# Moving half of a normalisation stage, and a bias preparation stage, into the projections beside them

## What is computed

```
for i in range(2):
    h = dilated_mixer(x, ...) if i == 0 else neighbourhood_mixer(x, ...)   # begins with x @ w_qkv
    x = layer_norm(ALPHA * x + h, ln_g[i, 0], ln_b[i, 0])
    f = hierarchical_moe(x, ...)
    x = layer_norm(ALPHA * x + f, ln_g[i, 1], ln_b[i, 1])                  # the closing stage
```

## Time and profile before

| what | us |
|---|---|
| median of 3 runs | 5646.84 |
| lowest and highest | 5639.95, 5656.57 |
| the profiled execution, its own time | 5643.55 |
| its span, first to last instruction | 5641.9 |
| `br`, first DMA issue to the first of `qa` | 12.0 |
| `a_sn`, first load issue to the first of `qb` | 66.6 |

### The profile page before, as it was taken

One profiled execution on the slowest core, in us unless ns is written; L12 is line 12 of the kernel. 1 busy time (PEld: TensorE's weight loads), 2 busy tenths in 40 slices (PEclk: granted clock), 3 DMA queues, 4 the chain that ended last, 5 costly groups with the idle time before them and its releaser, 6 DMA issues. The chain is left out here.

```text
span 5641.9 us, 110382 instructions
## 1 busy us (share of the span) xinstructions
PE 5159.5 (91%) x36030; PEld 4401.6 (78%) x36031; DVE 3861.8 (68%) x6739; ACT 2919.9 (52%) x4917; POOL 1161.2 (21%) x1032
## 2 busy tenths in 40 slices
PE   6999999999899988889999928998999897999993
PEld 5888798988889977778888827988888685888882
DVE  5678887687666658686877647775444555766886
ACT  3343444344388876455656434343777213644774
POOL 2010020000011110054544421100000002543552
PEclk9999999999999999989999969999999897999996
DMA  5877776465599977588988666664544436977996
GB/s 169 214 199 202 197 206 170 133 161 130 146 314 315 315 253 217 178 311 255 343 292 292 223 203 176 199 161 148 155 146 138 141 131 216 318 256 229 364 324 223
DMA packets 867118, 1236.12 MB, mean 219 GB/s; under 512 B 183102, under 2 KB 543981, under 8 KB 866732
## 3 DMA queue, kind: packets, MB, share of 16 engines
q1 hardware_dynamic: 739740, 883.58, 50.5%
q0 software_dynamic: 72272, 276.84, 16.1%
q10 hardware_dynamic: 54720, 70.60, 3.8%
HBM read 916.03 MB, written 333.67 MB: 222 GB/s over the span
## 5 line engine op out<-in xcount | busy, mean ns | idle before, releaser
L522 PE MATMUL qa_ps_out<-qa_x_hi,qa_w_hi 128*128 128x512 f32 x1344 | 534.3, 398 | 40.9 <-DVE qa_w_lo L646 23.8
L522 PE MATMUL qa_ps_out<-qa_x_lo,qa_w_hi 128*128 128x512 f32 x1344 | 529.8, 394 | 0.0
L522 PE MATMUL qa_ps_out<-qa_x_hi,qa_w_lo 128*128 128x512 f32 x1344 | 529.6, 394 | 0.0
L559 ACT ACTIVATE qa_w_hi<-qa_w_whole 128x1024 fp32r<-128x1024 f32 x180 | 191.2, 1062 | 456.9 <-DVE qa_w_whole L637 256.7
L522 PE MATMUL qa_ps_out<-qa_w_hi,qa_x_hi 128*128 128x256 f32 x1344 | 382.4, 284 | 5.6 <-DVE qa_w_lo L646 5.6
L522 PE MATMUL qa_ps_out<-qa_w_lo,qa_x_hi 128*128 128x256 f32 x1344 | 381.1, 284 | 0.0
L522 PE MATMUL qa_ps_out<-qa_w_hi,qa_x_lo 128*128 128x256 f32 x1344 | 381.0, 284 | 0.0
L2613 DVE CUSTOM_DVE_ANT_0 ga_minus_s<-ga_ps_s,ga_bias 128x512 f32<-128x512 f32 (+1 forms) x256 | 194.0, 758 | 257.6 <-PE ga_ps_s L2552 188.6
L1101 ACT ACTIVATE da_prob<-da_minus_s,da_rows 128x256 f32<-128x256 f32 (+1 forms) x768 | 317.9, 465 | 42.6 <-DVE da_rows L1069 42.4
L522 PEld LDWEIGHTS qa_ps_out<-qa_x_hi,qa_w_hi 128*128 128x128 f32 x1344 | 256.3, 191 | 101.0 <-DVE qa_w_lo L646 29.7
L1069 DVE CUSTOM_DVE_ANT_0 da_minus_s<-da_ps_s,da_bias 128x256 f32<-128x256 f32 (+1 forms) x768 | 259.6, 375 | 90.3 <-PE da_ps_s L1000 81.5
(11 more groups left out here) (490 smaller groups left out, 15427.3 us busy)
## 6 DMA issues: line engine op xcount, KB each, us to landing
a_ex_w_raw<-w SPq DMA_DIRECT2D x128, 1024.0 KB, 10.2
b_ex_w_raw<-w SPq DMA_DIRECT2D x128, 1024.0 KB, 10.3
qa_w_raw<-w_qkv_a SPq DMA_DIRECT2D x144, 512.0 KB, 4.2
a_ex_w_raw<-w POOLq DMA_DIRECT2D x66, 1024.0 KB, 9.8
b_ex_w_raw<-w POOLq DMA_DIRECT2D x66, 1024.0 KB, 8.2
da_q_cross<-qT SPq DMA_DIRECT2D x48, 1024.0 KB, 8.0
da_k_parts<-kT SPq DMA_DIRECT2D x48, 1024.0 KB, 10.2
a_mn_o_in<-o SPq DMA_DIRECT2D x16, 1584.0 KB, 8.6
```

The costliest lines, as they stand in the source:

```text
L522: done = pe.matmul(out, stationary, moving, start=(k == 0 and i == 0), stop=(k == KH - 1 and i == 2))
L559: act.activation(w_hi[:, p % W_RING], src, ACT.Copy).then_inc(w_hi_done, 1)
```

## The change

Four edits. (1) The stage `bias_rows` is gone; its two loads, three products, three copies and its store are done at the head of `qa`, with the projection's own result buffers `part` and `ps_out` as space; the first ScalarE copy into `part` waits for the store, and so does `diagonal_bias`. (2) In both projections two tiles are loaded and split ahead of the first weight block, the others behind it, on SP, ScalarE and VectorE. (3) `a_sn` does only the 8 tiles that pass 0 of `qb` reads; the 8 others are done within pass 0 of `qb`, one every three products from product 6 on, in the idle `x_rows`, through a ring of two slots; GpSimd issues their loads and stores and SP waits for the last store before it loads the first tile of pass 1. (4) In `merge_and_norm` `hi(0)` goes ahead of the last part of `w_o` (ahead of the last two in `b_mn`), and `lo(0)` stands right behind the first part.

```diff
+        def late_tile(p, step):
+            if not late or p < LATE_FIRST + step or (p - LATE_FIRST - step) % LATE_EVERY:
+                return None
+            i = (p - LATE_FIRST - step) // LATE_EVERY
+            return i if i < LATE else None
...
+                def late_load(i):
+                    rows = late.sums[bass.ts(late.tiles[i], P), :]
+                    pool.dma_start(late_rows[i % LATE_RING], rows).then_inc(late_loaded[i % LATE_RING], 16)
+
+                def norm_late_rows():
+                    pool.memset(late_power[:], -0.5).then_inc(late_ready, 1)
+                    pool.wait_ge(x_turned, TILES_OF_PASS)
+                    late_load(0)
+                    pool.dma_start(late_gain, row_broadcast(late.gain)).then_inc(late_const, 16)
+                    pool.dma_start(late_shift, row_broadcast(late.shift)).then_inc(late_const, 16)
+                    for i in range(1, LATE_RING):
+                        late_load(i)
+                    pool.wait_ge(late_ready, 1)
+                    for i in range(LATE):
+                        pool.wait_ge(late_widened, i + 1)
+                        pool.tensor_tensor(late_guess[:, i % 2], late_var[:, i % 2], late_power[:], ALU.pow
+                                           ).then_inc(late_guessed, 1)
+                        pool.wait_ge(late_done, i + 1)
+                        pool.dma_start(x[bass.ts(late.tiles[i], P), :], late_rows[i % LATE_RING]).then_inc(late_stored, 16)
+                        if i + LATE_RING < LATE:
+                            pool.wait_ge(late_stored, 16 * (i + 1))
+                            late_load(i + LATE_RING)
...
+                    if late and c == TILES_OF_PASS:
+                        sp.wait_ge(late_stored, 16 * LATE)
...
+                if bias:
+                    sp.dma_start(select, bias.c_bucket).then_inc(table_loaded, 16)
+                    sp.dma_start(table[0:N_BUCKETS, :], bias.t5_table).then_inc(table_loaded, 16)
+                for c in loads_at[None][:2]:
                     load_x(c)
                 load_w(0, 0)
                 load_w(0, 1)
+                for c in loads_at[None][2:]:
+                    load_x(c)
                 for c in loads_at[-1]:
                     load_x(c)
                 load_w(0, 2)
                 load_w(0, 3)
+                if bias:
+                    sp.wait_ge(rows_copied, N_DIL)
+                    sp.dma_start(bias.scratch.bias_rows, rows_of_bias).then_inc(rows_stored, 16)
...
+                if bias:
+                    pe.wait_ge(table_loaded, 32)
+                    pe.wait_ge(table_masked, 1)
+                    for g in range(N_DIL):
+                        pe.matmul(ps_out[0:HEADS, g, 0:REL_ROW], table, select[:, bass.ts(g, REL_ROW)], start=True,
+                                  stop=True).then_inc(rows_made, 1)
                 for c in tiles_at(-1):
                     turn(c)
+                if bias:
+                    pe.wait_ge(rows_copied, N_DIL)
...
+                    if bias and p == 0 and u == 0:
+                        act.wait_ge(rows_stored, 16)
...
+                for c in tiles_at(-1)[:2]:
+                    x_high(c)
                 w_high(0)
-                for c in tiles_at(-1):
+                for c in tiles_at(-1)[2:]:
                     x_high(c)
...
                     finish(p)
+                    if late_tile(p, 0) is not None:
+                        late_sum(late_tile(p, 0))
+                    if late_tile(p, 2) is not None:
+                        late_spread(late_tile(p, 2))
...
+                for c in tiles_at(-1)[:2]:
+                    x_low(c)
                 w_sum(0)
                 w_low(0)
-                for c in tiles_at(-1):
+                for c in tiles_at(-1)[2:]:
                     x_low(c)
...
                     mask_edge(p - 1)
+                    if late_tile(p, 1) is not None:
+                        late_middle(late_tile(p, 1))
+                    if late_tile(p, 3) is not None:
+                        late_shift_rows(late_tile(p, 3))
+                    if late_tile(p, 4) is not None:
+                        late_finish(late_tile(p, 4))
...
                 for i in range(W_PARTS):
+                    if i == W_PARTS - (1 if n_g > 1 else 2):
+                        hi(0)
                     ks = slice(WK * i, WK * i + WK)
                     act.wait_ge(w_loaded[i], 16)
                     act.activation(wo_hi[:, ks, :], w_raw[:, ks, :], ACT.Copy).then_inc(wo_hi_done, 1)
-                hi(0)
...
                     dve.tensor_tensor(wo_lo[:, ks, :], w_raw[:, ks, :], wo_hi[:, ks, :].bitcast(F32), ALU.subtract
                                       ).then_inc(wo_lo_done, 1)
-                lo(0)
+                    if i == 0:
+                        lo(0)
...
+        early_tiles, late_tiles = ([t for t in range(TILES) if t % SEQ_TILES // (SEQ_TILES // 2) == half] for half in range(2))
+        finish_layer("a", 0, N_DIL, a["x"], a["w_o_a"][0], scratch.x2, early_tiles)
```

More of the change, by code:

```diff
@@ L2283, in _, with sum_and_norm @@
                     pool.wait_ge(w2_loaded[i], 16 * (N_EXPERTS + 1))
-def sum_and_norm(nc, tag, gain, shift, out, scratch):
+def sum_and_norm(nc, tag, gain, shift, out, scratch, tiles=range(TILES)):
     RING = 6
+    N = len(tiles)
     with ExitStack() as ctx:
@@ L2337, in _ @@
                     load(t)
-                for t in range(TILES):
-                    if t + RING < TILES:
+                for t in range(N):
+                    if t + RING < N:
                         load(t + RING)
@@ L2374, in _ @@
                 add_up(0)
-                for t in range(TILES):
-                    if t + 1 < TILES:
+                for t in range(N):
+                    if t + 1 < N:
                         add_up(t + 1)
@@ L2436, in _ @@
                         finish(t - 1)
[L2437 removed]
+                finish(N - 1)
 def grid_attention(nc, ident, scratch):
@@ L2719, in build, with finish_layer @@
                        a["c_turns"])
-        def finish_layer(tag, layer, n_g, x, w_o, out):
+        def finish_layer(tag, layer, n_g, x, w_o, out, tiles=range(TILES)):
             with ExitStack() as ctx:
```

139 lines of the change are left out of this document (98 added, 41 removed).

## The result

The changed kernel takes 5601.62 us (median of 4 runs, 5599.79 to 5607.84) beside 5643.52 for the kernel before on the same chip: ratio 0.9924, 95% interval 0.9912 to 0.9936. Run again later beside another copy of the kernel before it took 5598.41 against 5648.82: 0.9910, interval 0.9896 to 0.9923. So the gain is 42 and 50 us by the medians, where the forecast was a time of 5598 and 47.4 us less than the profiled execution of before. From span to span (5641.9 to 5605.8) it is 36.1; the profiled execution of after, 5607.84 us, is the slowest of its four.

What follows compares the result with a forecast made beforehand. TensorE, busy 5159.5 of 5641.9 us, bounds the kernel; edits should cut its idle time. Terms -11.2 + 1 - 5 - 5 - 26.2 + 5 - 6 = -47.4 gave 5596 or 5599, stated as 5598; range 5589 to 5605.

Steps and rivals of the forecast that it cites:

- Bias stage: Program start: first load of `qa` moves from 17.89 to 6.7, gaining 11.2 us; bias products and first-tile wait are covered.
- Row store: Head of `qa`: ScalarE's first copy into `part` waits for the bias-row store, costing 0 to 4 us, taken as 1.
- Two tiles first: Starts of `qa` and `qb`: first product 15.5 to 16.5 us after first load, not 21.7; 5 us gained in each.
- The rival that the starts give little: Both projection starts: products 1 to 3 lose the gain, 2 us each instead of 5, time 5607; chance 0.13.
- Half of `a_sn`: In `a_sn`: eight tiles fewer at 3.28 us each save 26.2 us.
- Late work: Pass 0 of `qb`: VectorE at 96% and the two-slot ring's round trip of 9.2 us cost 5 us together, bounds 0 to 24.
- The throttled ring: Rival, pass 0 of `qb`: longer ring round trips cost TensorE 3 us per tile, 24 instead of 5, time 5617; chance 0.17.
- `b_mn`: Merge stage `b_mn`: project(0, 0) starts earlier and tile 1 follows at once, gaining 6 us, bounds 3 and 6.6.
- `a_mn`: Merge stage `a_mn`: earlier start, but tile 1 is merged as before and TensorE waits anyway; gain 0.
- The signs of being wrong: Late sums waiting over 5 us each for DMA, product 1 of either projection waiting longer, or an untouched stage changing length.

Runs made afterwards that it cites:

- without the late work: Changed kernel with all 16 tiles normalised in `a_sn` again and none in `qb`, the other three edits kept: 5618.81 us, ratio 0.9951 to the kernel before.
- the old merge: Changed kernel with `hi(0)` and `lo(0)` behind all four parts of `w_o` again in both merge stages: 5606.77 us, ratio 0.9933 to the kernel before.
- the narrow work: Changed kernel with VectorE's two wide instructions per late tile on 32 of 1024 columns, the rest left unnormalised: 5603.93 us, ratio 0.9930 to the kernel before.
- the third buffer: Changed kernel with three late row buffers instead of two, the unused output of ScalarE's sums going to PSUM: 5603.76 us, ratio 0.9923 to the kernel before.
- the failed move to GpSimd: Changed kernel with late tiles' gain multiplication moved from VectorE to GpSimd and mean subtraction on ScalarE: 5602.51 us, ratio 0.9918 to the kernel before.
- the third buffer and the multiplication on GpSimd: Changed kernel with three late row buffers, gain multiplication on GpSimd and mean subtraction on ScalarE: 5598.93 us, ratio 0.9917 to the kernel before.
- the other slots: Changed kernel with three late buffers, late tiles started at products 6, 9, 11, 13, 18, 20, 25 and 27: 5608.84 us, ratio 0.9923 to the kernel before.

## Why the prediction was right, and where its terms were off

The time, the range and the direction hold, and so does the mechanism of each edit but for two points below: how much load VectorE had, and where its margin was smallest. That the second median lies within 1 us of 5598 is luck: the two medians of the changed kernel differ by 3.2, the four of the kernel before by up to 5.6. (By its own parts the lower end of the range is 5590, not 5589.) Term by term:

- **Bias stage, -11.2:** measured 11.2 at the first load and 9.9 at product 0. That the bias products and the tile wait are covered is right; the two small loads cost the 1.3, of which I had counted only the two issues.
- **Row store, +1:** at most 0.4.
- **Two tiles first, -5 and -5:** 4.7 and 5.4 at product 0 (16.3 us after the first load; 15.5 to 16.5 forecast). That the DMA engines carry it was right. The rival that the starts give little isn't borne out: what `qb` lost again up to product 9 was 3.6 in the changed kernel but 0.0 without the late work and a gain of 3.8 with the old merge, whose code is the same there. It goes with the clock, which I hadn't in the sum: from its first load to product 9 `qb` has 34.6 us at the half level before; the four kernels with 40.3 to 40.8 lost 3.6 to 4.1, those with 22.8 to 30.6 lost nothing or gained up to 3.8. But part of the gain at product 0 is lost again by product 9, as the rival had it, though 1.2 us and not 3: the two kernels with new order and late work that have the half-clock time of before (34.5 and 34.6 us) reach product 9 4.3 and 4.1 us sooner after the first load, not 5.4.
- **Half of `a_sn`, -26.2:** 26.5.
- **Late work, +5 (0 to 24):** this term is the one mis-sized, 6.2 to 8.2 in five profiles that have it as it is. I had the right two causes and the right link ("hidden, unless VectorE is late too"), but expected most of the price from VectorE at 96%. Products 9 to 35, which hold all eight tiles, before and after:

```profile
3464.20:3613.60 149.40, 149.40 (x842) 131.63 (x841) 111.28 (x133) 57.64 (x80) 3.09 (x3) 1.00 0.60 165
```

```profile
3425.20:3580.40 155.20, 151.03 (x843) 131.63 (x842) 132.29 (x187) 72.79 (x110) 20.48 (x23) 1.00 0.68 197
```

  VectorE is busy for 85% of the stretch, and would be for 89% if TensorE's waits hadn't lengthened it. A late tile adds 2.6 us to its busy time (21.0 for eight), not 3.28: the durations of its instructions add up to 3.4, but in the rows one begins before the last has ended. Even so the margin at TensorE went: I had it smallest at product 31 and 5.6 us there; it was 6.7, because from product 28 on a product takes 5.76 us and not 5.45, and 6.4 at product 17. Either cause alone costs 0 (ring, shown by the narrow work) to 2.6 us (load, shown by the third buffer, 1.3 of it at the start of pass 1); together 7. The throttled ring, 24, stayed far off: from the issue of a store to the landing of the load behind it 8.7 to 10.8 us pass, against the 9.2 of the forecast, with 4.1 for the store and 4.7 for the load (medians from issue to landing in the 160 us), against 3.4 and 4.7 in the earlier trace rows.
- **`b_mn`, -6 (3 to 6.6):** 5.4, and 5.2 by undoing it. **`a_mn`, 0:** 0.
- **The signs of being wrong:** two of the three came true, product 1 waits 1.1 and 0.9 us longer, and `da`, which the diff doesn't touch, is 4.0 us longer. Neither upsets the sum, and the second was a poor sign: that stage, with the same code throughout, differs by 6.3 us between the twelve profiles and by 2.3 between the two of the changed kernel.

Of the missing 11.3 us in the profiled execution (47.4 less 36.1) 2.2 are the late work and 5.5 what was given back in `qa` after product 1 (1.9) and in `qb` up to product 9 (3.6). The rest is small in each place, and most of it lies in stages with unchanged code, `da` above all, whose length from the first to the last scores on VectorE was 530.4 to 536.7 us in the twelve profiles, 530.4 being that of the kernel before. Over runs this evens out: the medians say 42 and 50, and the rows without clock effects 11.2 - 1.3 + 4.7 + 5.4 + 26.5 - 7.2 + 5.4 = 44.7, or 1 less if the start of `qb` is taken at product 9.

GpSimd's part was as the Trainium skill, "SBUF — State Buffer", section "Who interferes with whom", has it: two engines that need the shared port wait for each other. In the changed kernel it is small. Its power of 128x1, shortest, median and longest in `a_sn` before, and mean beside the wide rows after:

```profile
L2351 POOL TENSOR_TENSOR a_sn_guess<-a_sn_var,a_sn_power x16: 547/548/585, 3304.7 to 3352.7; 128x1 f32<-128x1 f32 x16
```

```profile
L424 POOL TENSOR_TENSOR qb_late_guess<-qb_late_var,qb_late_power 128x1 f32<-128x1 f32 x7 | 10.7, 1529 | 40.4 <-DVE qb_late_var L832 40.4
```

Each is a microsecond longer, and each begins 0.2 us after a row instruction of VectorE (L836, 1.28 us) and ends behind it: GpSimd waits. VectorE's low parts keep a median of 1225. The same section's rule explains the failed move to GpSimd, where the trace agrees with both halves of it: instructions with two on-chip inputs are held, those with one in PSUM are not.

**Which version is best** the totals can't say: 5598.9 with the third buffer and the multiplication on GpSimd, 5603.8 with the third buffer alone and 5598.4 and 5601.6 for the changed kernel lie within their scatter. By the loss in pass 0 the third buffer is the better one, by 3.6 to 4.8 us against the four profiles without half clock there. The waits for low parts add up to 4.2 of the 7.2 us, with a fifth of 0.14 that the rows above leave out, and the extra wait at the transposes to 1.2; but the six products that begin late (22 to 24 and 29 to 31) are 5.7 us longer than before, so that each stop costs some 0.3 us more than its wait. Left open: why it does, and why the time at half clock differs from one execution to the next.

## What to carry to other kernels

Work moved beside a busy engine is free only if the waits around it are covered too: here a VectorE that is 88% busy was affordable and a ring of two was affordable, but not both, and a third buffer taken from PSUM that lay idle removed two thirds of the loss. Follow the margin of the operand that the bounding engine waits for, product by product, and not the share of busy time over the pass; and look at each queue that feeds it, for the other slots failed where two late tiles met on ScalarE, which had half its time to spare. Where an effect is smaller than the scatter of whole runs, compare the start times of one repeated instruction against those of the kernel before; the loss came out within 2 us of itself in five profiles while totals and stage lengths scattered by 5 to 16.

## What the runs showed of the hardware

- Taking 10 us off VectorE and giving the multiplication to GpSimd made the pass 4.0 us slower with three buffers and no faster with two: GpSimd needs 2.42 us for 128x1024 where VectorE needs 1.28, and VectorE's own instruction of two on-chip inputs stood for up to 2.55 us meanwhile (3778 against 1225 ns), 12.5 us in all.
- The time at half clock after a stage's start is not a property of the kernel: 27 to 58 us up to the end of `qa` in twelve profiles of nearly the same code, 34 and 44 in two of the very same kernel, and a microsecond of it goes with half a microsecond of length.
- A DMA of 512 KB issued by GpSimd took 4.1 us (store) and 4.7 us (load) to land, as medians, single stores 3.0 to 4.9, beside the projection's traffic (DMA engines 73% busy).
